# Rows of six token tiles loaded in halves over two DMA queues, with the first normalisation's engine queues ordered anew

## What is computed

```python
h = rmsnorm(x, norm_g)                        # x * rsqrt(mean(x*x) + eps) * g
proj = einsum('btd,dc->btc', h, w_in)         # 2048 -> 10240 columns
xa, za, v, bg, cg, zb, ga, gb = split(proj)
ya = pool_mixer(xa) * silu(za)
yb = bg * causal_conv3(cg * v) * silu(zb)
merged = sigmoid(ga + b) * (ya @ w_proj_pool) + sigmoid(gb + b) * (yb @ w_proj_conv)
y = rmsnorm(x + merged @ w_out, final_norm_g)
```

## Time and profile before

| | |
|---|---|
| Median of 3 runs | 2419.81 us (2419.48 to 2420.53) |
| The profiled execution's own time | 2420.62 us |
| Its span in the profile | 2418.8 us |
| TensorE busy | 2394.8 us (99%) |
| VectorE busy | 1693.0 us (70%) |
| ScalarE busy | 892.3 us (37%) |
| GpSimd busy | 116.5 us (5%) |
| Share of the chain that ended last | TensorE 98%, VectorE 1%, the rest below 1% each |

### The profile page before, as it was taken

The page is one execution under the profiler, slowest core; times in us unless marked ns, Lnnn a source line. Parts: engine busy times, 40 slices in busy tenths (PEclk is TensorE's granted clock), DMA queues, the critical chain, the costliest instruction groups (busy, mean ns, idle before and its releaser), DMA issues.

```text
span 2418.8 us, 42649 instructions
## 1 busy us (share of the span) xinstructions
PE 2394.8 (99%) x17822; PEld 2334.7 (97%) x17822; DVE 1693.0 (70%) x2316; ACT 892.3 (37%) x1303; POOL 116.5 (5%) x218
## 2 busy tenths in 40 slices
PE   7999999999999999999999999999999999999998
PEld 7999999999999999999999999999999999888886
DVE  6666666666666686777868777765755887887676
ACT  6433333333333443323322222233533533533535
POOL 3000000000000000000000000000000011100000
PEclk9999999999999999999999999999999999999999
DMA  6653323232333453433433433245655767898756
GB/s 215 217 200 127 127 90 127 90 120 97 113 104 109 160 208 134 166 138 135 165 132 113 136 132 135 97 168 204 226 168 164 277 246 280 289 350 302 248 177 227
DMA packets 195693, 418.04 MB, mean 173 GB/s; under 512 B 12489, under 2 KB 113917, under 8 KB 180656
## 3 DMA queue, kind: packets, MB, share of 16 engines
q1 hardware_dynamic: 170672, 284.85, 35.1%
q0 software_dynamic: 23744, 125.24, 13.7%
q10 hardware_dynamic: 1088, 5.24, 0.6%
HBM read 281.00 MB, written 133.77 MB: 171 GB/s over the span
## 4 chain that ended last, share of the span: by engine, by line
PE 98%; DVE 1%; issue 0%; ACT 0%; DMA 0%; POOL 0%; DVEq 0%; ACTq 0%; POOLq 0%
PE ps L1323 76%; PE ps L1450 12%; PE ps L1365 7%; PE ps L1472 1%; PE ps L1512 1%; PE ps L1488 1%; DMA xn<-in_x_prompt_dram 0%; DVE ops L2143 0%; DVE h0raw L2560 0%; DVE xn L2548 0%; ACT ops L1648 0%; ACT xn L1877 0%; ACT junk L1870 0%; DVE out L2406 0%; DVE out L2459 0%
## 5 line engine op out<-in xcount | busy, mean ns | idle before, releaser
L1323 PE MATMUL ps<-ops,hi 128*128 128x272 f32 x9824 | 1338.6, 288 | 0.2 <-DVE ops L2143 0.2
L1323 PEld LDWEIGHTS ps<-ops,hi 128*128 128x128 f32 x9824 | 1277.1, 188 | 0.7 <-DVE ops L2143 0.7
L1323 PE MATMUL ps<-ops,lo 128*128 128x272 f32 x4912 | 715.5, 288 | 0.0
L1323 PEld LDWEIGHTS ps<-ops,lo 128*128 128x128 f32 x4912 | 653.8, 188 | 0.0
L1573 ACT ACTIVATE hi<-sb 128x512 fp32r<-128x512 f32 x436 | 275.8, 633 | 578.0 <-PE ps L1323 447.8
L2123 DVE TENSOR_TENSOR pb<-pb,ps 128x544 f32<-128x544 f32 x336 | 241.7, 719 | 262.5 <-PE ps L1323 262.4
L1983 DVE TENSOR_TENSOR lo<-sb,hi 128x512 fp32r<-128x512 f32 x436 | 300.0, 688 | 154.5 <-ACT hi L1573 150.3
L1573 ACT ACTIVATE hi<-raw 128x512 fp32r<-128x512 f32 x265 | 167.5, 633 | 368.2 <-PE ps L1323 355.1
L1983 DVE TENSOR_TENSOR lo<-raw,hi 128x512 fp32r<-128x512 f32 x265 | 182.2, 688 | 112.2 <-ACT hi L1573 112.2
L1450 PE MATMUL ps<-ms_hi,mt 128*128 128x512 f32 x896 | 221.3, 389 | 0.0
L1450 PEld LDWEIGHTS ps<-ms_hi,mt 128*128 128x128 f32 x896 | 168.2, 188 | 34.8
(11 more groups left out here) (164 smaller groups left out, 1545.4 us busy)
## 6 DMA issues: line engine op xcount, KB each, us to landing
raw<-in_w_in_dram SPq DMA_DIRECT2D x157, 512.0 KB, 3.9
pb<-part SPq DMA_DIRECT2D x39, 1088.0 KB, 6.2
part<-pb POOLq DMA_DIRECT2D x37, 1088.0 KB, 5.3
mt_raw<-opq SPq DMA_DIRECT2D x28, 1024.0 KB, 6.2
gates<-pb POOLq DMA_DIRECT2D x16, 1088.0 KB, 8.4
gate<-gates SPq DMA_DIRECT2D x32, 544.0 KB, 6.2
ms<-in_w_out_dram SPq DMA_DIRECT2D x16, 1024.0 KB, 9.9
ops_raw<-opq SPq DMA_DIRECT2D x15, 1088.0 KB, 7.3
```

The costliest lines, as they stand in the source:

```text
L1323: mm = nc.tensor.matmul(ps[b][:, c, 0:HC], w[:, w_slot, kt * P:(kt + 1) * P], operand[:, kt, half, c * HC:(c + 1) * HC], start=fresh and k ...
```

## The change

Tiles 0 to 5 are all loaded in two halves of 1024 channels, one half on each queue. SyncE's queue becomes: halves of tiles 0, 1, 2, 3, 4, then weights 0, the half of tile 5, tile 7, further weights. ScalarE's queue becomes: halves of tiles 0 to 5, then tiles 6 and 8. Tile 1 is now scaled by VectorE, and the half (4, 1) is copied by VectorE. The orders of turns, squares, roundings, drains and copies are changed on ScalarE, VectorE, TensorE and GpSimd.

```diff
-        TURNS = ((0, 0), (0, 1), (1, 1), (1, 0), (3, 0), (2, 0), (4, 0), (2, 1), (3, 1),
-                 (5, 0), (5, 1), (7, 1), (7, 0), (8, 0), (8, 1), (6, 0), (4, 1), (6, 1))
+        HALVED = 6
+        TURNS = ((0, 1), (0, 0), (1, 0), (1, 1), (2, 0), (3, 0), (4, 0), (2, 1), (3, 1),
+                 (5, 0), (5, 1), (7, 0), (7, 1), (8, 1), (8, 0), (6, 0), (4, 1), (6, 1))
-        SQUARE_TURN = (0, 1, 3, 2, 4, 5, 7, 8, 6)
+        SQUARE_TURN = (0, 1, 2, 3, 4, 5, 7, 8, 6)
-        SCALED_ACT = (1, 5, 8, 6)
-        SCALED_DVE = (0, 3, 2, 4, 7)
-        COPIED_ACT = ((4, 1),)
+        SCALED_ACT = (5, 8, 6)
+        SCALED_DVE = (0, 1, 2, 3, 4, 7)
+        COPIED_ACT = ()
...
-            for t in (0, 1):
+            for t in range(HALVED):
                 sp.dma_start(xn[t][:, 0:D // 2], x_rows(t)[:, 0:D // 2]).then_inc(x_landed[t], 16)
-            for t in (3, 5):
-                sp.dma_start(xn[t][:, :], x_rows(t)).then_inc(x_landed[t], 16)
-            load_weights(0)
+                if t == HALVED - 2:
+                    load_weights(0)
             sp.dma_start(xn[7][:, :], x_rows(7)).then_inc(x_landed[7], 16)
...
             for i in range(11):
-                if i == 4:
+                if i == 3:
                     turn_vectors()
                 turn(i)
...
-            for t in (0, 1):
+            for t in range(HALVED):
                 act.dma_start(xn[t][:, D // 2:D], x_rows(t)[:, D // 2:D]).then_inc(x_landed[t], 16)
-            for t in range(2, TT, 2):
+            for t in (6, 8):
                 act.dma_start(xn[t][0:rows(t), :], x_rows(t)).then_inc(x_landed[t], 16)
...
             square(0)
             square(1)
-            scale(1)
+            square(2)
             square(3)
-            square(2)
             square(4)
             square(5)
+            split_hi(SLOT0)
             scale(5)
             first_operand_hi(0)
-            split_hi(SLOT0)
             split_hi(SLOT0 + 1)
             square(7)
...
             first_operand_hi(2)
+            drain(SLOT0 + 1)
             first_operand_hi(3)
-            drain(SLOT0 + 1)
-            copy_turned(4)
-            drain(SLOT0 + 2)
             split_hi(SLOT0 + 4)
             split_hi(SLOT0 + 5)
+            drain(SLOT0 + 2)
             first_operand_hi(4)
+            drain(SLOT0 + 3)
             split_hi(SLOT0 + 6)
-            drain(SLOT0 + 3)
             split_hi(SLOT0 + 7)
-            first_operand_hi(5)
             drain(SLOT0 + 4)
             drain(SLOT0 + 5)
             split_hi(NC * NQ)
+            first_operand_hi(5)
             first_operand_hi(6)
+            drain(SLOT0 + 6)
             split_hi(NC * NQ + 1)
             split_hi(NC * NQ + 2)
-            drain(SLOT0 + 6)
             first_operand_hi(7)
```

More of the change, by code:

```diff
@@ L1866, in square @@
                 r = rows(t)
[L1867 removed]
+                act.wait_ge(x_landed[t], 32 if t < HALVED else 16)
                 if SQUARED_AT[t] > 1:
@@ L2567, in _ @@
             nc.vector.tensor_copy(g_col[:, :], flat[0][:, 0:KD]).then_inc(g_made, 1)
+            scale(1)
+            copy_turned(TURNS.index((0, 1)))
             copy_turned(TURNS.index((0, 0)))
-            copy_turned(TURNS.index((0, 1)))
+            scale(2)
+            copy_turned(TURNS.index((1, 0)))
             copy_turned(TURNS.index((1, 1)))
-            copy_turned(TURNS.index((1, 0)))
+            copy_turned(TURNS.index((2, 0)))
             dve.wait_ge(setup_turned, 2)
@@ L2575, in _ @@
             scale(3)
-            scale(2)
+            scale(4)
             copy_turned(TURNS.index((3, 0)))
-            scale(4)
-            copy_turned(TURNS.index((2, 0)))
+            dve.wait_ge(setup_turned, 2)
+            nc.vector.tensor_copy(vec[:, :], flat[1][:, 0:NVEC]).then_inc(setup_copied, 1)
             copy_turned(TURNS.index((4, 0)))
@@ L2584, in _ @@
             split_lo(SLOT0)
-            dve.wait_ge(setup_turned, 2)
-            nc.vector.tensor_copy(vec[:, :], flat[1][:, 0:NVEC]).then_inc(setup_copied, 1)
+            split_lo(SLOT0 + 1)
             copy_turned(TURNS.index((5, 0)))
-            split_lo(SLOT0 + 1)
             scale(7)
@@ L2592, in _ @@
             split_lo(SLOT0 + 2)
+            copy_turned(TURNS.index((7, 0)))
             copy_turned(TURNS.index((7, 1)))
-            copy_turned(TURNS.index((7, 0)))
+            copy_turned(TURNS.index((8, 1)))
             copy_turned(TURNS.index((8, 0)))
-            copy_turned(TURNS.index((8, 1)))
             copy_turned(TURNS.index((6, 0)))
@@ L2599, in _ @@
             first_operand_lo(2)
+            copy_turned(TURNS.index((4, 1)))
             first_operand_lo(3)
+            split_lo(SLOT0 + 4)
             first_operand_sum(0)
-            copy_turned(TURNS.index((6, 1)))
-            split_lo(SLOT0 + 4)
             first_operand_sum(1)
+            first_operand_sum(2)
+            split_lo(SLOT0 + 5)
             first_operand_lo(4)
-            split_lo(SLOT0 + 5)
             split_lo(SLOT0 + 6)
             split_lo(SLOT0 + 7)
-            first_operand_sum(2)
+            copy_turned(TURNS.index((6, 1)))
             weight_sum(NC * NQ + 1)
+            weight_sum(NC * NQ + 2)
+            first_operand_sum(3)
+            first_operand_lo(5)
             split_lo(NC * NQ)
-            weight_sum(NC * NQ + 2)
-            first_operand_lo(5)
-            weight_sum(NC * NQ + 3)
+            first_operand_lo(6)
             split_lo(NC * NQ + 1)
-            first_operand_sum(3)
-            first_operand_lo(6)
             split_lo(NC * NQ + 2)
             first_operand_lo(7)
+            weight_sum(NC * NQ + 3)
             for s in range(NC * NQ, NS):
```

## The result

The changed kernel takes 2424.02 us, median of 22 runs (2423.0 to 2425.84); the kernel before, timed beside it, 2419.82 (2419.0 to 2420.6, 22 runs). The ratio is 1.0018, 95% interval 1.0012 to 1.0025: **4.2 us slower, 0.17%**, the interval reaching from 2.9 to 6.1 us. The profiled execution after took 2423.95 us, its span is 2422.1.

A forecast was written before the change was run, and what follows sets the result against it. TensorE's fixed list from 51.50 us was taken as the bound, so the start's delay counts: profiled 2420.62 plus 4.3 gives 2424.9, less 0.81 for the median, 2424.1 us; range 2419.4 to 2427.3.

The forecast's parts named there:

- The bound: TensorE from 51.50 us, in the fifth product: a fixed list; the change is worth what it moves that moment.
- The loads: DMA queues take turns by packet: tiles 2 and 4 land sooner, tile 5 at 26.9 us, 8.1 us later.
- ScalarE: Idle over 7 us before square(5); scale(5) runs 30.0 to 32.0, the first operand's remainder on VectorE ends at 36.4.
- VectorE and TensorE up to turn 8: VectorE's queue eats the earlier tiles' gain: turn 5 at 22.2, turns to 29.1, 0.2 us left.
- The clock term: After TensorE idles before turn 9: low clock from 32.0 to 37.1, first product's second group at 37.3, +4.3 us.
- my sum with the clock left high: First product's second group waits only for first_operand_lo(0), until 36.45: +3.4 us.
- The step from the profiled execution to the median: Whole kernel: the median of the runs lies 0.81 us below the profiled execution, giving 2424.1 us.
- The sum against the profile: Whole kernel: profiled execution of 2420.62 us plus 4.3 gives 2424.9 us.
- (a): Queues share by bytes, tile 5 lands by 24 us: 2419.8 us, no change; chance 0.18.
- (b): Late copy of (6, 1) delays a store to 72.3 to 84.1; with 20 us of store time 2428.6 us; chance 0.07.
- (c): Clock does not return under transposes, low for 5.1 us from the first product: +6.3, 2426.1 us; chance 0.05.
- (d): Faster: clock high through turns 5 to 8 and tile 5 early, at most some 5 us, 2415; chance 0.04.

The follow-up runs named there:

- after_again: The changed kernel, unchanged, run and profiled a second time: median 2424.23 us, profiled execution 2424.20 us.
- scale3_sooner: w0_behind_both with VectorE's scale(3) moved ahead of the copies of (1, 1) and (2, 0): 2418.77 us.
- filled_gap: The changed kernel with 28 unread transposes put into TensorE's idle stretch ahead of tile 5's turns: 2423.84 us.
- orders_only: The changed kernel's engine orders with the loads of the kernel before on both queues: 2422.5 us.
- t5_turns_later: The changed kernel's loads, with tile 5 squared, scaled and turned behind the start of the first product: 2423.78 us.
- w0_behind_both: The changed kernel with weights 0 loaded behind tile 5's half and ScalarE's split of weights 0 behind scale(5) and the operand's rounding: 2419.49 us.
- before_again: The kernel before, unchanged, run and profiled a second time: median 2419.86 us, profiled execution 2419.03 us.
- loads_only: The kernel before with only its loads changed to the halved ones, all engine orders kept: 2423.92 us.
- moved_and_scale3: The changed kernel with tiles 6 and 8 moved to SyncE's queue behind tile 7, together with the earlier scale(3) of scale3_sooner: 2419.03 us.

## Why the prediction was right, and which of its terms were not

The forecast was 2424.1 us, slower but most likely by no more than 0.2%; measured were 2424.02 and +0.17%. The prediction held that a change below 4.8 us can't be told from none; with 22 runs of each the interval is only some 1.6 us wide to either side, and sets the 4.2 apart from none. Point by point:

- **The bound.** That TensorE's list from the fifth product on is fixed held in every kernel (the table).
- **The loads.** Tiles 2, 3, 4 forecast at 12, 15.2, 17.4: squares at 12.5, 15.0, 17.3 (the 3 us put between tiles 2 and 3 did not follow from the sum's own 0.44 MB a us, which gives 2.3; measured are 2.5). Tile 5 forecast at 26.9: 27.0, and 26.5 in after_again. Weights 0 1.2 us ahead: 1.3. The argument that the same set has been moved by then as when weights 0 landed before was tested twice: swap the two and the other lands at 27.0; take tiles 6 and 8 off the set and it lands at 21.4. The Trainium skill's rule of turns at packet boundaries (DMA: Bandwidth & Descriptors, "Queues, rings and completion order") was confirmed with 175 to 177 packets.
- **ScalarE.** scale(5) forecast 30.0 to 32.0: 29.96 to 31.96. The remainder's end forecast 36.4: it started at 33.89 and takes 2.42, so 36.3. Not foreseen: with eight loads to issue in place of six, ScalarE's first square began at 6.44 and not at 5.70. It cost nothing that shows: the turn of tile 3 came when it was forecast (next point).
- **VectorE and TensorE up to turn 8.** That VectorE's queue eats the head start of the early tiles was right (turn 5 forecast for 22.2, it came at 21.93), and scale3_sooner shows it from the other side. That turns 6 to 8 run at the low clock until 29.1 was not: it was back by 26 and the turns ended at 27.9. It cost nothing, since tile 5 was later still.
- **The clock term was mis-sized, and its source misread.** I took 5.1 us of low clock from 32.0 on, and +4.3. The 5.1 us was the stretch from 24.11, "when work resumed". But the clock was low long before that (before; columns as in the earlier trace rows):

```profile
17.00:20.00 3.00, 0.82 (x10) 0.73 (x9) 2.58 (x4) 1.56 (x3) 1.66 (x2) 0.82 1.03 420
20.00:24.00 4.00, 3.34 (x16) 2.78 (x14) 3.64 (x4) 3.60 (x4) 0.96 (x3) 0.50 1.03 261
```

  In finer slices the granted clock fell at 18.9, while TensorE stood idle ahead of 19.64, and rose at 29.15: 10.2 us, not 5.1. No trace has a low stretch of 5.1 us. In the changed kernel's profile it lasted 3.4 us, to 35.4, and the price was 3.3 us, the value of my sum with the clock left high, +3.4. filled_gap shows that in this case the clock is covered by the operand's remainder. In after_again it was low from 29.7 to 36.6 and did show: the second group came some 0.8 us behind the remainder's end, 0.3 us later than in the first profile although tile 5 was there 0.5 us sooner.
- **The step from the profiled execution to the median** was the other error, of the same size and the other sign. I took the profiled execution of before as 0.81 us above the median and subtracted that from the sum, as if it lay outside the stretch in question. It lay inside: that execution had the clock low for longer than most. Its 33.05 was a late draw, the changed kernel's 36.35 an ordinary one (2423.95 against a median of 2424.02). By the invariant of the table the median execution of before starts its fifth product at 49.4, the median one after at 53.6: 4.2 us, of which 3.3 are between the two profiles and 0.8 is the first profile's late draw. The sum against the profile, 2424.9, was 0.95 too high for the profiled execution after (2423.95), and the 0.81 that I took off from there should have been 0.07 added, 0.88 the other way. The mechanism was right, and so was the size that it has with the clock left high, +3.4 us against 3.3; that 2424.1 hit to 0.1 us was luck.
- **Rivals.** (a) By bytes: refuted by 175 to 177 packets, and by 27.0 us. (b) The late store: GpSimd issued it at 71.70 (forecast 72.3), it had landed by 81.8 (forecast 84.1), and no wait of TensorE followed. (c) The clock rose while TensorE did nothing but transposes in the changed kernel too, at 25.1 us; the Trainium skill's sentence on transposes (TensorE: Matmul & The Clock Gate, "Part 4: PE-mode transpose") does not hold for these float32 ones. (d) Not seen in these two kernels.

Three expectations behind the prediction missed by more: orders_only (+1.0 expected, +2.8 measured), where I had followed ScalarE and forgotten the order of landings on VectorE; t5_turns_later, where I had counted on 1 to 3 us; and w0_behind_both, whose gain of 1.4 us did not come.

## What to carry to other kernels

A load with short packets is not only slow by itself when another queue carries long ones: it holds back whatever is queued behind it too. Here its 32 packets an engine outlasted the 20 that the other queue had left, so the half tile behind it waited for all of them; put what is needed first ahead of such a load, or keep the other queue short (27.0 against 21.4 us here). Before reordering loads, write down which set of transfers must have been moved when the awaited one lands; with the two loads in either order, the last of the set landed at 27.0 here. And when an effect is as small as the spread of the runs, look in the profile for a point after which nothing differs, and compare that: the sum against one profiled execution is no better than that execution's own draw.

## What the runs showed of the hardware that I had not expected

One program, run again and with its rows scaled within some 0.1 us of the same times up to tile 4, differs by 1.6 us in its start by when the clock comes back alone. After the same idle stretch of 2.18 us ahead of the turn at 19.6 or 19.7, the granted clock was at 0.50 until about 29.2 in one execution and until about 22.6 in the other. The spread of this kernel's runs (2419.0 to 2420.6 in the first 22, 2419.0 to 2420.8 in before_again) is about that wide.

In all seven profiled executions with a wait of 2.72 us before tile 3's turn at about 22 us, the clock fell to 1.2 GHz during that wait or within 1 us after it (20.5 to 22.9 us), and it came back between 25 and 28.1 us. In orders_only, where that wait is at 25.02, the clock had fallen at 19.9, in a wait of 2.95 us ahead of another turn; in loads_only it fell at 21.4, in a wait of 0.91 us that came after one of 1.92. With waits of 0.90, 1.49 and 1.38 us (scale3_sooner) it stayed high. Whether it does so in every execution of that kernel I did not try.

The granted clock of the first microseconds does not fit the durations: in moved_and_scale3 it reads 1.00 throughout, yet the 24 transposes from 17.63 took 0.21 us each, as long as those at 0.50 elsewhere, and in the changed kernel the first 24, from 10.74, took 0.20 us each at 1.00. I read it as a level that the trace does not yet know, and go by the durations there; no run settles it.

No kernel here beats the kernel before by what can be measured: scale3_sooner, the best, is 0.98 us below it (2418.77 against 2419.75), well within its interval.
